# Splitting the first cross-attention weight chunk ahead, into places that are free early

## The reference

```python
mix = jnp.concatenate([a, r], axis=-1) @ w_out[l]
x = x + rms_norm(mix, norm_mix_post[l])
h = rms_norm(x, norm_xa_pre[l])
mn = rms_norm(mem, norm_mem[l])
q = (h @ xa_wq[l]).reshape(B, S, XA_HEADS, XA_HEAD_DIM)
kv = (mn @ xa_wkv[l]).reshape(B, M, 2, XA_HEADS, XA_HEAD_DIM)
s = jnp.einsum('bshd,bmhd->bhsm', q, kv[:, :, 0]).astype(jnp.float32) * (XA_HEAD_DIM ** -0.5)
p = jax.nn.softmax(s, axis=-1).astype(x.dtype)
xo = jnp.einsum('bhsm,bmhd->bshd', p, kv[:, :, 1]).reshape(B, S, D_MODEL) @ xa_wo[l]
```

## Time and profile before

| | |
|---|---|
| median of 3 runs | 1443.06 us (1442.0 to 1444.55) |
| the profiled execution | 1443.56 us, of which its span is 1441.7 us |
| mean granted TensorE clock of the span | 0.998 of full speed |
| busy, share of the span | PE 97%, weight loads 80%, DVE 59%, POOL 57%, ACT 44% |
| chain of waits by engine | PE 80%, DVE 6%, DMA 4%, POOL 4%, ACT 3% |
| DMA | 172.17 MB, mean 119 GB/s |

### The profile page before, as it was taken

The page is one execution under the profiler, slowest core; times in us unless marked ns, Lnnn a source line. Parts: engine busy times, 40 slices in busy tenths (PEclk is TensorE's granted clock), DMA queues, the critical chain, the costliest instruction groups (busy, mean ns, idle before and its releaser), DMA issues.

```text
span 1441.7 us, 18923 instructions
## 1 busy us (share of the span) xinstructions
PE 1400.5 (97%) x6744; PEld 1150.8 (80%) x6744; DVE 849.3 (59%) x1277; ACT 641.2 (44%) x1299; POOL 817.4 (57%) x575
## 2 busy tenths in 40 slices
PE   7999999998999989999999999999999999999998
PEld 7988888666978768888788788888888888868886
DVE  5799996886865667755255743332333333343868
ACT  6422233676433655244456433333333333534454
POOL 1587264003771466520344687777777774699753
PEclk9999999999999999999999999999999999999999
DMA  5576132200043264310436133333323324933363
GB/s 197 170 250 230 50 98 59 59 2 1 30 152 111 77 245 147 95 52 0 149 121 224 56 110 110 106 99 107 104 97 110 110 81 161 364 89 94 103 210 149
DMA packets 127309, 172.17 MB, mean 119 GB/s; under 512 B 9584, under 2 KB 73328, under 8 KB 127216
## 3 DMA queue, kind: packets, MB, share of 16 engines
q1 hardware_dynamic: 123776, 161.52, 33.9%
q10 hardware_dynamic: 3440, 9.45, 1.8%
HBM read 129.77 MB, written 41.16 MB: 119 GB/s over the span
## 4 chain that ended last, share of the span: by engine, by line
PE 80%; DVE 6%; DMA 4%; POOL 4%; ACT 3%; issue 2%; SPq 0%; POOLq 0%; ACTq 0%; DVEq 0%
PE ps L1108 24%; PE ps L1110 23%; PE ps L1109 23%; PE ps L1104 4%; PE ps L1505 2%; DVE z L2788 1%; DMA raw<-in_xa_wkv_dram 1%; PE ps L1276 1%; PE ps L1370 1%; POOL wd L1077 1%; PE ps L1304 1%; DMA gain_b<-f_rows 1%; POOL w_lo L981 1%; PE ps L1348 1%; DVE sm L2663 1%
## 5 line engine op out<-in xcount | busy, mean ns | idle before, releaser
L1108 PE MATMUL ps<-w_hi,t_hi 128*128 128x512 f32 (+2 forms) x592 | 229.2, 387 | 4.5 <-POOL w_lo L997 2.8
L1110 PE MATMUL ps<-w_hi,t_lo 128*128 128x512 f32 (+2 forms) x592 | 226.4, 382 | 0.0
L1109 PE MATMUL ps<-w_lo,t_hi 128*128 128x512 f32 (+2 forms) x592 | 224.8, 380 | 0.0
L1108 PEld LDWEIGHTS ps<-w_hi,t_hi 128*128 128x128 f32 x592 | 112.4, 190 | 24.0 <-POOL w_lo L997 3.5
L913 POOL TENSOR_TENSOR w_lo<-raw,w_hi 128x512 fp32r<-128x512 f32 (+1 forms) x52 | 78.9, 1525 | 90.4 <-ACT w_hi L1791 90.4
L1110 PEld LDWEIGHTS ps<-w_hi,t_lo 128*128 128x128 f32 x592 | 112.1, 189 | 20.4
L1109 PEld LDWEIGHTS ps<-w_lo,t_hi 128*128 128x128 f32 x592 | 112.4, 190 | 19.3
L997 POOL TENSOR_TENSOR w_lo<-raw,w_hi 128x512 fp32r<-128x512 f32 x32 | 41.7, 1312 | 104.0 <-ACT w_hi L2144 104.0
L3111 DVE TENSOR_TENSOR ev<-ps,ev 128x512 f32<-128x512 f32 x21 | 14.5, 692 | 143.7 <-PE ps L1110 143.7
L1791 ACT ACTIVATE w_hi<-raw 128x512 fp32r<-128x512 f32 (+1 forms) x52 | 31.6, 619 | 107.4 <-PE ps L1110 67.4
L2337 ACT ACTIVATE ev<-ps 128x512 f32<-128x512 f32 x63 | 37.7, 598 | 88.1 <-PE ps L1110 88.1
(11 more groups left out here) (360 smaller groups left out, 4105.2 us busy)
## 6 DMA issues: line engine op xcount, KB each, us to landing
raw_a<-in_ffn_w_gu_dram SPq DMA_DIRECT2D x44, 256.0 KB, 3.1
raw_b<-in_ffn_w_gu_dram SPq DMA_DIRECT2D x44, 256.0 KB, 3.2
f_rows<-fs SPq DMA_DIRECT2D x44, 256.0 KB, 3.7
gain_b<-f_rows SPq DMA_DIRECT2D x39, 256.0 KB, 2.7
tables<-f_rows SPq DMA_DIRECT2D x38, 256.0 KB, 2.7
f_rows<-fa SPq DMA_DIRECT2D x33, 256.0 KB, 3.4
raw<-in_xa_wkv_dram SPq DMA_DIRECT2D x32, 256.0 KB, 3.7
raw<-in_xa_wo_dram SPq DMA_DIRECT2D x32, 256.0 KB, 2.6
```

The lines of the kernel that those rows point to most:

```text
L1108: nc.tensor.matmul(out, a_hi, b_hi, start=start, stop=False, skip_group_check=onto)
L1109: nc.tensor.matmul(out, a_hi, b_lo, start=False, stop=False, skip_group_check=onto)
L1110: return nc.tensor.matmul(out, a_lo, b_hi, start=False, stop=stop, skip_group_check=onto)
```

## The change

It does four things. The first chunk's units 0 to 7 are split while the output projection still runs: their high and low parts go into the token places `t_hi[:, k, 0:512]` and `t_lo[:, k, 0:512]` of the tiles 0 to 3, once `last_piece` has finished these tiles (`first_units` on ACT, in pieces between its other work, and eight subtractions at the head of POOL's list). Units 8 to 11 use `w_hi` and `w_lo`, units 12 to 15 the places `w_hi2` and `w_lo2` (`kv_beside`), units 16 on the ring again. DVE's units 2, 6, 10 and 14 go to POOL, so that DVE has the units 18, 22, 26 and 30 alone. And ACT's roundings are placed anew: four fewer ahead of chunk 1's copies, with the copies of the keys (L2060) ahead of the roundings of units 24 to 27.

```diff
--- before.py
+++ after.py
@@ -135,7 +135,17 @@
 
 def kv_on_dve(n):
 
-    return n % RING == 2
+    return n >= 2 * NK and n % RING == 2
+
+
+def kv_lows(n):
+
+    return n // RING - 3
+
+
+def kv_beside(n):
+
+    return NK + RING <= n < 2 * NK
 
 
 def H2_HI(t):
@@ -585,6 +595,10 @@
             c = slice(m * P, (m + 1) * P)
             return high[:, :, c], low[:, :, c]
 
+        def memory_slots(n):
+
+            return (w_hi2, w_lo2) if kv_beside(n) else (w_hi, w_lo)
+
         def tile_at(v):
 
             return (v + 4) % NT
@@ -739,7 +753,7 @@
                 c, k = divmod(n, NK)
                 dst, src = raw[:, k % RING, :], wkv_v[k, :, c * 512:(c + 1) * 512]
                 if n >= RING and kv_on_dve(n - RING):
-                    sp.wait_ge(kv_low, n // RING)
+                    sp.wait_ge(kv_low, kv_lows(n - RING))
                     sp.dma_start(dst, src).then_inc(w_loaded[k % RING], 16)
                 else:
                     load(U_KV + c * NK, k, dst, src)
@@ -975,13 +989,18 @@
             def mem_low(n):
 
                 k = n % RING
-                pool.wait_ge(mem_rounded, n + 1)
+                pool.wait_ge(mem_rounded, n - NK + 1)
                 if n and kv_on_dve(n - 1):
-                    pool.wait_ge(kv_low, n // RING + 1)
-                nc.gpsimd.tensor_tensor(w_lo[:, k, :], raw[:, k, :], w_hi[:, k, :].bitcast(F32),
+                    pool.wait_ge(kv_low, kv_lows(n - 1))
+                hi, lo = memory_slots(n)
+                nc.gpsimd.tensor_tensor(lo[:, k, :], raw[:, k, :], hi[:, k, :].bitcast(F32),
                                         ALU.subtract).then_inc(w_split, 2 if n and kv_on_dve(n - 1) else 1)
 
-            for n in range(4 * NK):
+            for k in range(NK):
+                pool.wait_ge(w_rounded, U_KV - RING + k + 1)
+                nc.gpsimd.tensor_tensor(t_lo[:, k, 0:512], raw[:, k % RING, :], t_hi[:, k, 0:512].bitcast(F32),
+                                        ALU.subtract).then_inc(w_split, 1)
+            for n in range(NK, 4 * NK):
                 if not kv_on_dve(n):
                     mem_low(n)
             for n in range(7 * RING):
@@ -1441,13 +1460,21 @@
             def kv_ready(n):
 
                 if kv_on_dve(n):
-                    pe.wait_ge(kv_low, n // RING + 1)
+                    pe.wait_ge(kv_low, kv_lows(n))
                 else:
                     pe.wait_ge(w_split, U_KV + n + 1)
 
+            def memory_rows(c):
+
+                def operands(k, t):
+                    hi, lo = memory_slots(c * NK + k)
+                    weights = (hi[:, k % RING, :], lo[:, k % RING, :]) if c else (t_hi[:, k, 0:512], t_lo[:, k, 0:512])
+                    return m_hi[:, k, t * P:(t + 1) * P], m_lo[:, k, t * P:(t + 1) * P], *weights
+                return operands
+
             for c in range(4):
                 product(c * NK + U_KV, NM, 512, lambda t: pe.wait_ge(act_ev, kv_seen(c - 2, t)) if c >= 2 else None,
-                        rows_by_weights(m_hi, m_lo, 512), b0=2 * (c % 2), ready=lambda k: kv_ready(c * NK + k),
+                        memory_rows(c), b0=2 * (c % 2), ready=lambda k: kv_ready(c * NK + k),
                         between=turn_keys if c == 2 else lambda: None)
                 if c == 0:
                     pe.wait_ge(act_ev, ACT_EV["h2"])
@@ -1996,11 +2023,17 @@
             def round_units(n):
 
                 nonlocal rounds
-                for _ in range(min(n, 4 * NK - rounds)):
-                    u, slot = U_KV + rounds, (U_KV + rounds) % RING
+                for _ in range(min(n, 3 * NK - rounds)):
+                    u, slot = U_KV + NK + rounds, (U_KV + NK + rounds) % RING
                     act.wait_ge(w_loaded[slot], 16 * (u // RING))
-                    act.wait_ge(w_used, u - RING + 1 if rounds >= RING else u - NK + 1)
-                    nc.scalar.activation(w_hi[:, slot, :], raw[:, slot, :], ACT.Copy).then_inc(mem_rounded, 1)
+                    if rounds < RING:
+                        act.wait_ge(w_used, u - 2 * NK + 1)
+                    elif kv_beside(NK + rounds):
+                        act.wait_ge(w_used, U_KV)
+                    else:
+                        act.wait_ge(w_used, u - (NK if rounds < 3 * RING else RING) + 1)
+                    nc.scalar.activation(memory_slots(NK + rounds)[0][:, slot, :], raw[:, slot, :],
+                                         ACT.Copy).then_inc(mem_rounded, 1)
                     rounds += 1
 
             def sums(*steps):
@@ -2025,6 +2058,13 @@
                 tile_ready("o", 1, t, NT, U_O + NK)
                 nc.scalar.activation(y[:, t, 512:1024], bank(t), ACT.Copy).then_inc(act_ev, 1)
 
+            def first_units(*units):
+
+                for k in units:
+                    act.wait_ge(w_loaded[k % RING], 16 * ((U_KV + k) // RING))
+                    act.wait_ge(tile_done, TILES["o"] + NT - 1 + 4)
+                    nc.scalar.activation(t_hi[:, k, 0:512], raw[:, k % RING, :], ACT.Copy).then_inc(w_rounded, 1)
+
             upper_out(0)
             sums(("post", 0))
             upper_out(1)
@@ -2032,21 +2072,27 @@
             upper_out(2)
             sums(("post", 2), ("pre", 1))
             upper_out(3)
+            first_units(0, 1, 2)
             sums(("post", 3))
             upper_out(4)
+            first_units(3)
             sums(("post", 4), ("pre", 2))
+            first_units(4)
             mem_high(0)
+            first_units(5)
             upper_out(5)
             sums(("post", 5))
+            first_units(6)
             mem_high(1)
+            first_units(7)
             upper_out(6)
             sums(("post", 6), ("pre", 3))
             round_units(RING)
             upper_out(7)
             sums(("post", 7), ("pre", 4))
-            round_units(RING)
+            round_units(2)
             sums(("pre", 5))
-            round_units(RING)
+            round_units(2)
             def q_round(n):
 
                 act.wait_ge(w_loaded[n % RING], 16 * ((U_Q + n) // RING))
@@ -2059,6 +2105,7 @@
                         act.wait_ge(turned, TURNED_K + i + 1)
                         nc.scalar.activation(kM[:, 2 * i:2 * i + 2, :], bank(4 + i).rearrange("p (k m) -> p k m", k=2),
                                              ACT.Copy).then_inc(act_ev, 1)
+                    round_units(RING)
                 if c == 3:
                     for n in range(3):
                         q_round(n)
@@ -2077,11 +2124,10 @@
                 for t in (2 * c, 2 * c + 1):
                     hi_parts(h2_turned(t), t_hi, t * P)
                 if c == 0:
-                    round_units(RING)
                     sums(("pre", 7))
                     round_units(RING)
                 else:
-                    round_units(NK)
+                    round_units(RING)
             act.wait_ge(added, NT)
             act.dma_start(gain_a[:, :], rows(norm_xa_post)).then_inc(ga_in, 16)
             act.wait_ge(scaled, 2 * NT + NM)
@@ -2850,7 +2896,7 @@
             def kv_unit_low(n):
 
                 k = n % RING
-                dve.wait_ge(mem_rounded, n + 1)
+                dve.wait_ge(mem_rounded, n - NK + 1)
                 nc.vector.tensor_tensor(w_lo[:, k, :], raw[:, k, :], w_hi[:, k, :].bitcast(F32),
                                         ALU.subtract).then_inc(kv_low, 1)
 
@@ -2871,15 +2917,11 @@
             post_rows(4)
             post_rows(5)
             pre_rows(3)
-            kv_unit_low(2)
             post_rows(6)
-            kv_unit_low(6)
             post_rows(7)
-            kv_unit_low(10)
             row_lows(0)
             row_lows(1)
             pre_rows(4)
-            kv_unit_low(14)
             pre_rows(5)
             kv_unit_low(18)
             row_lows(2)
```

## The result

The changed kernel takes 1433.5 us (median of 4 runs, 1432.29 to 1433.89) against 1443.65 us for the kernel before beside it; the ratio is 0.9929, interval [0.9917, 0.994]. The forecast was 1433.7 us. The profiled execution took 1433.89 us with a span of 1431.7 us, 10.0 us less than before.

What follows compares the result with a forecast made beforehand. PE was taken as the bound, busy 97% of the span, losing 10.03 us in chunks 0 to 2. Taking 9.5 us from 1443.56 gives 1434.1, less 0.5 for the median: 1433.7 us, range 1432.0 to 1439.0.

Steps and rivals of the forecast that it cites:

- template of 12.74 us a chunk: Last stretch, chunk 3 of the memory product, where PE loses nothing: 48 matmuls and 16 transposes, used to price the others.
- 10.03 us found: PE's loss against the full last stretch: 2.02 us in chunk 0, 3.13 in chunk 1, 4.88 in chunk 2.
- changes of place: Where units switch buffers, waits of a tenth of a microsecond were expected to stay, so 9.5 us was taken.
- a ring of loads: Memory product: load of 4.71 us, ACT rounding, DVE and POOL subtractions, then the next load; four places, no lead.
- The lead: Splitting chunk 0 early puts the ring two rounds ahead, 14.8 us, more than the 10.0 us lost.
- The old pace leads by 6 us: Cross-check: five rounds of 7.4 us from 492.6 end at 529.6 us; PE wants the last unit at 536.
- ACT's eight roundings at no cost: Between 463.3 and 481 us, 5.1 us of moved roundings fit ACT's 8.7 us idle, delaying copies under 1 us.
- The rival that ends slower: A late first unit on ACT delays the memory product's start past 7 us of cover: 1446 to 1448 us, chance 0.05.
- The rule on the shared interface: POOL and DVE contend for SBUF, so low parts of units 8 to 15 might be slow, costing 1.5 us in chunk 2.
- the slow end: POOL's longest subtraction, 2.37 us, for all of units 8 to 15: 19 us, unit 15 done at 504.1.
- Slack: Margin before PE wants a low part: 3.5 us at unit 19, 1.7 us at unit 28, the tightest.
- The keys: Chunk 2: copying the keys ahead of the roundings of units 24 to 27 removes PE's wait of 2.5 us.

Runs made afterwards that it cites:

- e3: Changed kernel, but units 12 to 15 use the ring's places instead of their own; stage 55.72 us against 52.56, ratio to the kernel before 0.994.
- e5: Changed kernel with only units 0 to 3 split ahead, units 4 to 7 from 484.4 us; stage 55.37 us, ratio to the kernel before 0.9921.
- e7: e5 with DVE's unit 18 put ahead of the second token tile instead of behind it; stage 55.61 us, ratio to the kernel before 0.994.
- e4: Changed kernel without splitting the first chunk ahead, its roundings starting at 484.4 us; stage 61.02 us, ratio to the kernel before 0.9966.
- e6: Changed kernel with the low parts of units 10 and 14 on DVE again instead of POOL; stage 55.20 us, ratio to the kernel before 0.9933.
- e1: Kernel before, with only the copies of the keys moved ahead of the roundings of units 24 to 27; ratio to the kernel before 0.9983.
- e2: Changed kernel with the copies of the keys behind the roundings of units 24 to 27 again; stage 54.26 us, ratio to the kernel before 0.9923.

## Why the prediction was right, point by point

- **What bounds.** The template of 12.74 us a chunk held: 12.55 to 12.76 us, and 14.50 with the keys. Of the 10.03 us found, all came (10.12). I had kept back 0.5 us for the changes of place; there was nothing to keep.
- **The number.** That the forecast of 1433.7 us came within 0.2 us is in part luck. The gain was 10.15 us for 9.5, and the median of the kernel before had moved up by 0.6 us, from 1443.06 to 1443.65, which made up for it. The sum itself, 1434.1 less 0.5, gives 1433.6.
- **What the ring is.** The prediction reads the earlier trace rows as a ring of loads, "each load's latency is seen". In chunk 0 the chain is that. In chunk 1 and the start of chunk 2 the same chain of the kernel before takes 17.8 us from one rounding to the next (501.11 to 518.88), of which one load is 5.05 us, DVE's lows and token tile 6.5, ACT's part ahead of them 3.2 and POOL 2.4:

```profile
504.60 2.48 DVE t_lo L2480 x4
507.19 1.80 DVE y L2820
509.01 1.65 DVE y L2828
510.67 0.61 DVE w_lo L2854
511.44 2.37 POOL w_lo L981
513.83 5.05 DMA raw<-in_xa_wkv_dram
```

The lead covers both, so the forecast stood; the losses of e3, e5 and e7 ran along this longer path.
- **The lead.** e4 shows that it is the main term: 8.46 us by the stage, some 5 by the times. "The old pace leads by 6 us", worked out from 7.4 us a round, rests on a slip: at 492.6 us POOL ended its fourth subtraction, and that is unit 4's, since DVE makes unit 2. Unit 3's low part was there by about 491.1, as the load into its place went at 491.18. By my estimate from these rows a round is then 7.6 us, the lead 5 us, and half the lead 2 us short, where e5's stage lost 2.8. But the shortage came in chunk 2, over ACT's list, DVE's tiles and loads beside the stores, not at the last unit.
- **ACT's eight roundings at no cost.** POOL had unit 7 at 481.1 (at most 481.4 forecast); DVE's last `m_lo` ended at 480.1, 7 us early. The rival that ends slower had its full cover.
- **Places of their own.** Given as slack only; e3 puts a price on them, 3.16 us in the stage, by way of ACT's list.
- **DVE's units to POOL.** I booked this as relief of DVE. It is also a load on POOL, whose 1.85 us a unit is more than PE's 1.38 (e4); with the lead it is right to do it, since the alternation costs 2.64 us in the stage (e6).
- **The rule on the shared interface.** The trace agrees with the Trainium skill, GPSIMD Engine Reference, section Key points, that the two engines contend: the eight low parts of 8 to 15 took 15.01 us, 1.88 each, beside DVE's token work, against 1.30 for the shortest, as unit 7's above. That is 4 us less than the 19 us of the slow end. They were done at 501.1, a little later than the 499 forecast and 8.5 us before PE wanted unit 15, and it cost nothing.
- **Slack.** Unit 19 was split at 511.5 and wanted at 516.8: 5.3 us, forecast 3.5. Unit 28 at 531.2, wanted at 532.7: 1.5 us, forecast 1.7. It remains the tightest place of those I worked out.
- **The keys.** Worth 2.5 us alone (e1) and 1.7 us in the stage with the rest (e2). The 2.5 us of the earlier trace rows were the right term.
- **PE's pace from the token places.** 48 matmuls of chunk 0 took 498.25 - 487.37 = 10.88 us, 0.227 us each, for the 0.231 forecast: no slower.

The parts do not add up. Removed singly they cost 8.46, 3.16, 2.64 and 1.70 us of stage, together more than the 10.12 us there were. The likely reason is that each of the later three covers places in chunks 1 and 2 that a shorter lead lays open too; no run removes two of them at once. Of the four only the lead is also clear in the times of whole runs. What stays open is how the losses of chunk 2 in e3, e4 and e5 divide between ACT's list, DVE's list and the loads beside the stores; e7 moved one unit on DVE's list and met the next wait on the same list.

## What to carry to other kernels

The ring of loads with four places and no lead passed late loads, the stores beside them and the in-order waits of three engines on to PE; look for when its first unit is made, and for places that fall free before the stage begins. A stretch in which PE loses nothing is the template by which the others are to be priced. When a transfer or an operation is moved, follow what stands behind its new place in the queue: a lead can pay for it, an order alone often moves the wait.

## What the runs showed of the hardware

POOL's subtraction of 128x512 fp32 took 1.3 us at best and 1.85 to 1.88 us on average while DVE worked on token tiles (e4 and the changed kernel). The slowing goes both ways: DVE's sum of 128x1024 took 1.23 us or 2.20 us, and its subtraction of 128x512 took 0.61 us in the chain of e5 and 1.72 in that of e7. A 256 KB load took 3.3 us in the median of the changed kernel's stage, 5.3 us in the median among the 512 KB stores of e7, and 7.07 us once there. Matmuls whose weights lie in the token places ran at 0.227 us each, the others at 0.231.
